# Second attention of a two-layer encoder step: the diagonal mask moves from VectorE's product and the second accumulation into the score accumulation on TensorE

## The chip, the cores and the metric

One core of a Trainium2 chip (trn2). The metric is the device time of one execution in microseconds: the median of several runs, lower is better. The kernel before takes 2124.3 us (median of 3 runs, 2124.23 to 2124.6).

## The reference

One inference step of a two-layer encoder over 1024 prompt rows and 32 sample rows (which see 512 cached rows), width 1024. Layer 0 uses differential attention, layer 1 stick-breaking attention. After each comes an output projection, a gated per-layer embedding, and at the end one rmsnorm. All arithmetic is float32. The change touches only the attention of layer 1, for 16 heads of 64:

```python
def block(qb, qpb):
    z = jnp.einsum('bqhd,bkhd->bhqk', qb.astype(f32), kf) * (B_DH ** -0.5)
    valid = k_pos[None, :] < qpb[:, None]
    log_keep = jnp.where(valid, jax.nn.log_sigmoid(-z), 0.0)
    after = lax.cumsum(log_keep, axis=3, reverse=True) - log_keep
    a = jnp.where(valid, jnp.exp(jax.nn.log_sigmoid(z) + after), 0.0)
    return jnp.einsum('bhqk,bkhd->bqhd', a, vf)
```

A weight is exp(z - the sum of softplus(z) over this key and all later valid ones), and a query sees only keys strictly ahead of it.

## The kernel before, in words

The program runs in phases: a norm, the first attention (names with the prefix la), a mixing phase (mix_a), the second attention (`stick_layer`, prefix lb), a second mixing phase (mix_b). Each phase gives every engine its own hand-written list of instructions, tied together by counting semaphores; there is no scheduler.

`stick_layer` works through eight groups of two heads. Groups 0 to 6 are a hardware loop, group 7 is written out behind it. In a group the keys lie on the 128 partitions and the queries in the free dimension. The work goes by **pairs** (c, b): query chunk c (0 and 1: 512 prompt queries each; 2: the 32 sample rows) against key block b of 128 keys. The order is (0,0) to (0,3), (1,0), (2,0), (1,1) to (1,7), thirteen pairs; a pair has one **unit** for each of the two heads, the sample pair one unit for both. A pair is diagonal where some of its queries lie inside the key block: (0,0) to (0,3) and (1,4) to (1,7). Such a pair computes only the columns from the block on (512, 384, 256 and 128 of them), and its first 128 columns need the strict mask. So 8 x 2 = 16 units of a group are diagonal, and 128 in all.

A unit goes round the engines so:

- TensorE, `scores` (L1496 on, matmul at L1529; sample pair L1520): three products (high x high, low x high, high x low) of 64-row operands, term by term, and within a term head 0 and then head 1. The result is z in a PSUM bank of lb_sc. The semaphore z is raised per head at its last term.
- VectorE, `clamp` (L1286): min(z, 40) into lb_m. ScalarE, `exp` and `log` (L1132, L1137): ln(1 + exp).
- VectorE, `softplus`: max(z, that) into lb_s (L1299), the softplus. In a diagonal unit a second instruction multiplies the first 128 columns by the 0/1 matrix `strict` (L1305), behind a semaphore from the first; in the sample unit it is `strict_sample` (L1310), ahead of sums over the key blocks in lb_rs (L1313, L1316). Then `split` makes a high part (the cast, L1336) and a low part (L1338).
- TensorE, `after`: in a diagonal unit first the **hide** matmul (L1548; sample L1542), which adds -1e30 to the masked entries of z by unit x hide on the full 128 x 128 array; then two triangle matmuls (L1551), which subtract the sums of the softplus. It waits for the semaphore soft ahead of the hide and for low ahead of the triangles. `column_sums` (L1562) adds up a pair's whole softplus.
- ScalarE, `weights` (L1147): exp of the bank into lb_a. TensorE, `values` (L1587; sample L1581): the products with v. VectorE, `add` (L1355), and GpSimd, a scaling by what the block keeps (L1457), gather them in lb_o.

The order on TensorE in step i is: scores of pair i, values of pair i-2, after and column sums of pair i-1, and then, in most steps, a piece of projection (L105): the last token tiles of this group (steps 0 to 2), with small transposes (L1494), the gate (steps 3 to 5), or the first token tiles of the next group (from step 6). VectorE in step i: the clamps of pair i, add of pair i-2, softplus and split of pair i, then gate work, splits of the next group's weights (L1265, steps 3 and 5; L1270) and of turned tiles (L1275). At a group's end come the last add and `finish` (L1365), and then the loop's branch. In group 7 the splits of weights are replaced by splits of the next phase's operand (L1203 on ScalarE, L1407 on VectorE).

SP issues the loads and stores; the mask tables are loaded once, at the start of the program.

In the listing, `views(s)` gives a unit's bank and buffers, `span(c, b)` the first column of a pair, their number, and whether it is diagonal.

Of the kernel before, what the change touches and what calls it, by code (L numbers as in the profile page):

```python
# [27 lines left out]
P = 128  # L28
# [890 lines left out]
def stick_layer(nc, top, name, h, w_in, k_past, v_past, k_out, v_out, o_dram, w_out, ident, masks, stage, norm):  # L919
# [29 lines left out]
        q = max(0, b * P - c * QC)  # L949
        return q, QC - q, b >= 4 * c  # L950

    diagonal = sum(c < 2 and b >= 4 * c for c, b, _ in UNITS)
    with ExitStack() as ctx:
        sb = lambda n, s, dt=F32: ctx.enter_context(nc.sbuf_tensor(f"{name}_{n}", s, dt))
        pb = lambda n, s: ctx.enter_context(nc.psum_tensor(f"{name}_{n}", s, F32))
# [17 lines left out]
                     turned=9, turned_high=9, turned_low=9, past_turned=1, past_high=1, past_low=1,  # L973
                     tok_stored=64, g_ready=3, g_normed=3, g_clamped=3, g_exp=3, g_log=3, g_soft=3, g_sig=3, g_done=3,
                     z=N, clamped=N, exp=N, log=N, soft=N, high=SPLIT, low=SPLIT, after=N, a=N, sums=CARRIED,
                     keep=CARRIED, scaled=CARRIED, added=NP - 1, sampled=1, pv=NP, dve_link=diagonal + 5, o_ready=3,
                     pe_tick=0, fill=1, pads=1)
        table.update({f"w_loaded{s}": 16 * KT // STAGES for s in range(STAGES)})
        table.update({f"o_stored{c}": 16 for c in range(3)})
# [265 lines left out]
        def _(dve):  # L1245
# [32 lines left out]
            def body(r, more):  # L1278
# [7 lines left out]
                    dve.tensor_scalar(x, slot, SOFT_MAX, None, ALU.min).then_inc(S["clamped"], 1)  # L1286

                def softplus(s):
                    c, b, _ = UNITS[s]
                    slot, x, sp, _ = views(s)  # L1290
                    dve.wait_ge(S["log"], at.next("log"))

                    if s < 2:
                        dve.wait_ge(S["low"], at.before("low"))
                    elif UNITS[s - 2][0] == 2:
                        dve.wait_ge(S["after"], at.nth("after", s - 1))
                    else:
                        dve.wait_ge(S["low"], at.nth("low", split_before(s - 1)))
                    ins = dve.tensor_tensor(sp, slot, x, ALU.max)  # L1299
                    if c < 2 and not span(c, b)[2]:  # L1300
                        ins.then_inc(S["soft"], 1)
                    elif c < 2:
                        ins.then_inc(S["dve_link"], 1)
                        dve.wait_ge(S["dve_link"], at.next("dve_link"))
                        dve.tensor_tensor(sp[:, 0:P], sp[:, 0:P], masks["strict"][:, :], ALU.mult).then_inc(S["soft"], 1)  # L1305
                    else:
                        ins.then_inc(S["dve_link"], 1)
                        dve.wait_ge(S["dve_link"], at.next("dve_link"))
                        new = sp[:, :, PB * DEC:]
                        dve.tensor_tensor(new, new, masks["strict_sample"][:, :, :], ALU.mult).then_inc(S["dve_link"], 1)  # L1310
                        dve.wait_ge(S["dve_link"], at.next("dve_link"))
                        dve.wait_ge(S["after"], at.nth("after", s))
                        dve.tensor_copy(rs[:, :, PB - 1, :], new).then_inc(S["dve_link"], 1)  # L1313
                        dve.wait_ge(S["dve_link"], at.next("dve_link"))
                        for b in reversed(range(PB - 1)):
                            ins = dve.tensor_tensor(rs[:, :, b, :], rs[:, :, b + 1, :], sp[:, :, (b + 1) * DEC:(b + 2) * DEC],  # L1316
                                                    ALU.add)
                            if b:
                                ins.then_inc(S["dve_link"], 1)
                                dve.wait_ge(S["dve_link"], at.next("dve_link"))  # L1320
                            else:
                                ins.then_inc(S["soft"], 1)
# [149 lines left out]
        def _(pe):  # L1472
# [24 lines left out]
            def body(r, more):  # L1497
                at, ahead = Count(table, r), Count(table, r + 1)

                def scores(i):  # L1500
                    c, b = PAIRS[i]
                    if i >= 2:
                        pe.wait_ge(S["a"], at.nth("a", through(i - 2)))
                    else:
                        pe.wait_ge(S["a"], at.before("a"))
                    if i == 0:
                        pe.wait_ge(S["turned_low"], at.nth("turned_low", 4))
                    if (c, b) == (1, 0):
                        pe.wait_ge(S["turned_low"], at.nth("turned_low", NT))
                    if c == 2:  # L1510
                        pe.wait_ge(S["turned_low"], at.all("turned_low"))
                        pe.wait_ge(S["past_low"], at.all("past_low"))
                        high, low = qk
                        slot = views(units(i)[0])[0]
                        for b in range(SB):
                            for n, (x, y) in enumerate(((0, high), (1, high), (0, low))):
                                for hd in range(2):
                                    f = slice(hd * DH, (hd + 1) * DH)
                                    keys = kpt[x][f, b * P:(b + 1) * P] if b < PB else qk[x][f, 1, SEQ:]
                                    last = pe.matmul(slot[:, hd, b * DEC:(b + 1) * DEC], keys, y[f, 0, SEQ:ROWS],  # L1520
                                                     start=b == 0 and n == 0, stop=n == 2, skip_group_check=True)
                        last.then_inc(S["z"], 1)
                        return
                    q = span(c, b)[0]
                    high, low = qk
                    for n, (x, y) in enumerate(((high, high), (low, high), (high, low))):
                        for s in units(i):
                            f = slice(UNITS[s][2] * DH, (UNITS[s][2] + 1) * DH)
                            last = pe.matmul(bank(s)[:, q:], x[f, 1, b * P:(b + 1) * P],  # L1529
                                             y[f, 0, c * QC + q:(c + 1) * QC], start=n == 0, stop=n == 2,  # L1530
                                             skip_group_check=True)
                            if n == 2:
                                last.then_inc(S["z"], 1)

                def after(s):
# [3 lines left out]
                    pe.wait_ge(S["soft"], at.nth("soft", s + 1))  # L1539
                    if c == 2:  # L1540
                        for hd in range(2):
                            pe.matmul(slot[:, hd, PB * DEC:], unit[:, :], hide[:, 0:DEC], **add)  # L1542
                            pe.matmul(slot[:, hd, 0:PB * DEC], masks["neg_ones"][:, :],
                                      rs[:, hd].rearrange("p b n -> p (b n)"), **add)
                            last = pe.matmul(slot[:, hd, :], masks["neg_tri"][:, :], sp[:, hd, :], **add)
                    else:
                        if span(c, b)[2]:
                            pe.matmul(slot[:, 0:P], unit[:, :], hide[:, :], **add)  # L1548
                        pe.wait_ge(S["low"], at.nth("low", split_before(s) + 1))
                        for part in halves(s):  # L1550
                            last = pe.matmul(slot, tri[:, :], part, **add)  # L1551
# [629 lines left out]
def build(nc, A, out):  # L2181
# [3 lines left out]
    with top:  # L2185
# [2 lines left out]
        o_dram = internal("o_t", (GROUPS, P, ROWS))  # L2188
        ident = top.enter_context(nc.sbuf_tensor("ident", [P, P], F32))
        masks = {n: top.enter_context(nc.sbuf_tensor(n, s, F32)) for n, s in  # L2190
                 (("neg_tri", [P, P]), ("neg_ones", [P, P]), ("strict", [P, P]), ("strict_sample", [P, 2, DEC]))}
        h_offset = -(-nc.sbuf_base // 32) * 32
        h = [top.enter_context(nc.sbuf_tensor(f"h_{n}", [P, KT, ROWS], F32R)) for n in ("high", "low")]
        stage = top.enter_context(nc.sbuf_tensor("stage", [P, STAGE], F32))
# [74 lines left out]
```

## Time and profile before

| | us |
|---|---|
| median of 3 runs | 2124.3 (2124.23 to 2124.6) |
| the profiled execution | 2126.75 |
| its span in the profile | 2125.0 |
| TensorE busy | 1911.1 |
| VectorE busy | 1255.2 |
| ScalarE busy | 1005.7 |
| GpSimd busy | 323.0 |

The mean granted clock of TensorE in this execution is 0.957 of full speed. Times in the profile count from the start of the span. A timeline row gives the start, the duration, the engine, the line, the operation and its operands; a bracket at its end is the engine's idle time before it and what ended it. Durations of matmuls hold their latency, so that neighbours overlap; what one costs in a dense stretch is the step from its start to the next one's. "x2" is two instructions merged into one row.

### The profile page before, as it was taken

The numbers are of one execution on the slowest core, as the hardware profiler recorded it, in microseconds if no ns is written. First come the engines' busy times: TensorE is split into PE (matmuls) and PEld (weight loads), VectorE is DVE, ScalarE is ACT, GpSimd is POOL, SyncE is SP. The second block draws the span as 40 slices with busy tenths as digits, with TensorE's granted clock in tenths as the row PEclk, the third lists the DMA queues.
The fourth block names the chain that finished last, engine by engine and source line by source line (L and its number), as shares of the span: only waits on it lengthen the run. The fifth ranks groups of instructions, "written<-read, shape, count | busy, mean of one in ns | idle before, by whom it ended". The sixth has DMA issues, their size and how long they took to land. (4 is left out here: it accounts for less than half of the span.)

```text
span 2125.0 us, 35549 instructions
## 1 busy us (share of the span) xinstructions
PE 1911.1 (90%) x11420; PEld 1637.2 (77%) x11420; DVE 1255.2 (59%) x2661; ACT 1005.7 (47%) x2361; POOL 323.0 (15%) x541
## 2 busy tenths in 40 slices
PE   3999989999899889996799999999999999689995
PEld 2877878878778689986777777777777778479995
DVE  4456555564554622454286868686868686844455
ACT  5455454554554622454254555454545454522345
POOL 0111111111111000264010101110101011100341
PEclk7999999999999889998999999999999999979999
DMA  4121111211111232211111111010111111133213
GB/s 130 51 63 49 48 45 56 60 35 45 55 56 49 92 104 84 70 64 57 36 46 36 45 35 55 26 55 25 55 35 45 44 37 46 72 101 96 63 47 122
DMA packets 161891, 124.22 MB, mean 58 GB/s; under 512 B 11136, under 2 KB 152768, under 8 KB 161792
## 3 DMA queue, kind: packets, MB, share of 16 engines
q1 hardware_dynamic: 161792, 123.08, 18.8%
q8 instruction: 40, 0.66, 0.1%
q14 instruction: 59, 0.48, 0.1%
HBM read 89.53 MB, written 33.52 MB: 58 GB/s over the span
## 5 line engine op out<-in xcount | busy, mean ns | idle before, releaser
L105 PE MATMUL lb_pj<-lb_w_high,h_high 128*128 128x384 f32 (+1 forms) x576 | 209.1, 363 | 19.4 <-DVE lb_w_low L1265 10.3
L105 PE MATMUL la_pj<-la_w_high,h_high 128*128 128x384 f32 (+1 forms) x576 | 208.0, 361 | 6.9 <-DVE la_w_low L569 6.9
L1132 ACT ACTIVATE lb_m<-lb_m 128x512 f32<-128x512 f32 (+4 forms) x200 | 98.8, 521 | 236.5 <-DVE lb_m L1286 235.3
L105 PE MATMUL lb_pj<-lb_w_high,h_low 128*128 128x384 f32 (+1 forms) x576 | 200.8, 349 | 0.0
L105 PE MATMUL lb_pj<-lb_w_low,h_high 128*128 128x384 f32 (+1 forms) x576 | 200.0, 347 | 0.0
L105 PE MATMUL la_pj<-la_w_low,h_high 128*128 128x384 f32 (+1 forms) x576 | 195.9, 340 | 0.0
L105 PE MATMUL la_pj<-la_w_high,h_low 128*128 128x384 f32 (+1 forms) x576 | 195.0, 339 | 0.0
L1457 POOL TENSOR_TENSOR lb_o<-lb_o,lb_keep 128x512 f32<-128x512 f32 (+3 forms) x80 | 77.3, 967 | 649.0 <-ACT lb_keep L1156 649.0
L1299 DVE TENSOR_TENSOR lb_s<-lb_sc,lb_m 128x512 f32<-128x512 f32 (+4 forms) x200 | 110.1, 550 | 61.3 <-ACT lb_m L1137 61.2
L418 ACT ACTIVATE la_p<-la_sc,la_nm 128x128 f32<-128x128 f32 (+5 forms) x144 | 106.1, 739 | 57.8 <-DVE la_nm L608 56.0
L105 PEld LDWEIGHTS lb_pj<-lb_w_high,h_high 128*128 128x128 f32 (+1 forms) x576 | 108.4, 188 | 29.4 <-issue 11.7
L1286 DVE TENSOR_SCALAR lb_m<-lb_sc 128x512 f32<-128x512 f32 (+4 forms) x200 | 101.4, 547 | 38.5 <-PE lb_sc L1529 23.0
L1338 DVE TENSOR_TENSOR lb_s_low<-lb_s,lb_s_high 128x512 fp32r<-128x512 f32 (+1 forms) x192 | 113.7, 592 | 6.6
L105 PEld LDWEIGHTS la_pj<-la_w_high,h_high 128*128 128x128 f32 (+1 forms) x576 | 105.3, 183 | 12.6 <-issue 6.8
L105 PEld LDWEIGHTS lb_pj<-lb_w_high,h_low 128*128 128x128 f32 (+1 forms) x576 | 108.5, 188 | 5.8
L105 PEld LDWEIGHTS lb_pj<-lb_w_low,h_high 128*128 128x128 f32 (+1 forms) x576 | 107.8, 187 | 4.3
L606 DVE TENSOR_REDUCE la_mx<-la_sc 128x1 f32<-128x128 f32 (+5 forms) x144 | 107.6, 747 | 3.1 <-DVE la_sc L601 0.2
L105 PEld LDWEIGHTS la_pj<-la_w_low,h_high 128*128 128x128 f32 (+1 forms) x576 | 104.4, 181 | 4.3
L105 PEld LDWEIGHTS la_pj<-la_w_high,h_low 128*128 128x128 f32 (+1 forms) x576 | 105.0, 182 | 3.2
L1551 PE MATMUL lb_sc<-lb_s_high,lb_tri 128*128 128x512 f32 (+1 forms) x192 | 79.5, 414 | 28.5 <-DVE lb_s_low L1338 28.5
L1336 DVE CAST lb_s_high<-lb_s 128x512 fp32r<-128x512 f32 (+1 forms) x192 | 79.8, 416 | 25.1
L1137 ACT ACTIVATE lb_m<-lb_m 128x512 f32<-128x512 f32 (+4 forms) x200 | 92.3, 507 | 0.3
(295 smaller groups left out, 5197.4 us busy)
## 6 DMA issues: line engine op xcount, KB each, us to landing
stage<-in_a_w_in SPq DMA_DIRECT2D x60, 192.0 KB, 3.1
stage<-in_b_w_in SPq DMA_DIRECT2D x60, 192.0 KB, 2.9
stage<-in_ple_w_gate SPq DMA_DIRECT2D x22, 512.0 KB, 3.6
h_low<-o_t SPq DMA_DIRECT2D x14, 528.0 KB, 6.5
mix_b_xs<-x_mid SPq DMA_DIRECT2D x8, 528.0 KB
norm_a_xt<-in_x SPq DMA_DIRECT2D x8, 512.0 KB, 3.6
stage<-in_a_w_in SPq DMA_DIRECT2D x16, 256.0 KB, 5.2
out_ak<-la_tok SPq DMA_DIRECT2D x8, 512.0 KB, 3.3
```

What stands on the lines that cost most here:

```text
L105: last = pe.matmul(out, x, y, start=start and n == 0, stop=stop and n == 2, **kw)
L418: act.activation(p[c][u % (3 - c)][0:n, 0:nk], scores_of(u)[:, c, :], ACT.Exp, bias=nm[0:n, u % 2, c:c + 1], accum_out=sums[0:n, u % 2, c: ...
L606: dve.reduce_max(mx[0:n, u % 2, c:c + 1], x[:, c, :], AX.X).then_inc(S["dve_link"], 1)
L1132: act.activation(x, x, ACT.Exp).then_inc(S["exp"], 1)
L1137: act.activation(x, x, ACT.Ln, bias=1.0).then_inc(S["log"], 1)
L1286: dve.tensor_scalar(x, slot, SOFT_MAX, None, ALU.min).then_inc(S["clamped"], 1)
L1299: ins = dve.tensor_tensor(sp, slot, x, ALU.max)
L1336: dve.tensor_copy(high, sp).then_inc(S["high"], 1)
L1338: dve.tensor_tensor(low, sp, high.bitcast(F32), ALU.subtract).then_inc(S["low"], 1)
L1457: pool.tensor_tensor(out, out, kept[n % 2][:, q:], ALU.mult).then_inc(S["scaled"], 1)
L1551: last = pe.matmul(slot, tri[:, :], part, **add)
```

## The change

The hide matmul moves. For a diagonal pair it is issued in `scores`, for each head right after that head's last term, ahead of the semaphore z; for the sample pair both follow the last score matmul. So z is already about -1e30 in masked entries when it is clamped: exp gives 0, the logarithm 0, and the max 0, which is what the product gave. The products with `strict` and `strict_sample` go, with the semaphore step between max and product, and so does the table `strict_sample`. `after` no longer issues the hide. The numbers of hide matmuls, 128 and 16, stay the same.

```diff
--- before.py
+++ after.py
@@ softplus(s), VectorE
-                    c, b, _ = UNITS[s]
+                    c = UNITS[s][0]
                     slot, x, sp, _ = views(s)
...
                     ins = dve.tensor_tensor(sp, slot, x, ALU.max)
-                    if c < 2 and not span(c, b)[2]:
+                    if c < 2:
                         ins.then_inc(S["soft"], 1)
-                    elif c < 2:
-                        ins.then_inc(S["dve_link"], 1)
-                        dve.wait_ge(S["dve_link"], at.next("dve_link"))
-                        dve.tensor_tensor(sp[:, 0:P], sp[:, 0:P], masks["strict"][:, :], ALU.mult).then_inc(S["soft"], 1)
                     else:
                         ins.then_inc(S["dve_link"], 1)
                         dve.wait_ge(S["dve_link"], at.next("dve_link"))
                         new = sp[:, :, PB * DEC:]
-                        dve.tensor_tensor(new, new, masks["strict_sample"][:, :, :], ALU.mult).then_inc(S["dve_link"], 1)
-                        dve.wait_ge(S["dve_link"], at.next("dve_link"))
                         dve.wait_ge(S["after"], at.nth("after", s))
@@ body(r, more), TensorE
+                masked = dict(start=False, stop=True, skip_group_check=True)
+
                 def scores(i):
...
                                     last = pe.matmul(slot[:, hd, b * DEC:(b + 1) * DEC], keys, y[f, 0, SEQ:ROWS],
                                                      start=b == 0 and n == 0, stop=n == 2, skip_group_check=True)
+                        for hd in range(2):
+                            last = pe.matmul(slot[:, hd, PB * DEC:], unit[:, :], hide[:, 0:DEC], **masked)
                         last.then_inc(S["z"], 1)
                         return
...
                             if n == 2:
+                                if span(c, b)[2]:
+                                    last = pe.matmul(views(s)[0][:, 0:P], unit[:, :], hide[:, :], **masked)
                                 last.then_inc(S["z"], 1)
@@ after(s), TensorE
                     if c == 2:
                         for hd in range(2):
-                            pe.matmul(slot[:, hd, PB * DEC:], unit[:, :], hide[:, 0:DEC], **add)
...
                     else:
-                        if span(c, b)[2]:
-                            pe.matmul(slot[:, 0:P], unit[:, :], hide[:, :], **add)
                         pe.wait_ge(S["low"], at.nth("low", split_before(s) + 1))
```

The rest of the diff is the count of the semaphore dve_link (four steps a group instead of 16 + 5) and the list of mask tables.

## Rows read from the trace of the kernel before

**Rows 1.** The page of the kernel before: busy time of each engine.

```profile
PE 1911.1 (90%) x11420; PEld 1637.2 (77%) x11420; DVE 1255.2 (59%) x2661; ACT 1005.7 (47%) x2361; POOL 323.0 (15%) x541
```

**Rows 2.** Windows, us: PE, PEld, DVE, ACT, POOL busy; granted clock; DMA share; GB/s.

```profile
1140.00:1240.00 100.00, 94.26 (x568) 75.16 (x567) 75.17 (x159) 53.85 (x131) 11.59 (x12) 0.97 0.14 43
1155.00:1170.00 15.00, 11.90 (x53) 9.53 (x50) 10.27 (x23) 5.89 (x16) 0.00 (x0) 0.77 0.10 30
1260.00:1275.00 15.00, 12.15 (x59) 9.90 (x60) 11.39 (x26) 7.06 (x20) 0.00 (x0) 0.89 0.06 20
...
1778.00:1793.00 15.00, 14.04 (x85) 10.71 (x82) 12.55 (x30) 7.70 (x20) 1.03 (x1) 1.00 0.10 26
1840.00:1880.00 40.00, 22.59 (x92) 15.00 (x91) 29.96 (x60) 20.49 (x41) 5.00 (x5) 0.69 0.15 47
```

**Rows 3.** Waits from 1040 to 1880 us: us in total, times, longest.

```profile
PE lb_sc L1551 <- DVE lb_s_low L1338: 28.5, 31, 1.1
```

**Rows 4.** Timeline of TensorE, heads of groups 2 and 7: start us, us.

```profile
1260.76 0.33 PE L1548 MATMUL lb_sc<-lb_hide,lb_unit 128*128 128x128 f32 x1 [1.11 <-DVE lb_s L1305]
1262.02 0.50 PE L1551 MATMUL lb_sc<-lb_s_high,lb_tri 128*128 128x512 f32 x1 [0.93 <-DVE lb_s_low L1338]
...
1264.23 0.50 PE L1551 MATMUL lb_sc<-lb_s_high,lb_tri 128*128 128x512 f32 x1 [0.96 <-DVE lb_s_low L1338]
...
1264.87 0.53 PE L105 MATMUL lb_pj<-lb_w_high,h_high 128*128 128x384 f32 x1
1265.19 0.53 PE L105 MATMUL lb_pj<-lb_w_high,h_low 128*128 128x384 f32 x1
...
1780.32 0.50 PE L1551 MATMUL lb_sc<-lb_s_high,lb_tri 128*128 128x512 f32 x1 [0.96 <-DVE lb_s_low L1338]
```

**Rows 5.** Timeline of VectorE at the head of group 2.

```profile
1257.09 1.29 DVE L1286 TENSOR_SCALAR lb_m<-lb_sc 128x512 f32<-128x512 f32 x2 [2.52 <-issue]
1259.69 0.69 DVE L1299 TENSOR_TENSOR lb_s<-lb_sc,lb_m 128x512 f32<-128x512 f32 x1 [1.32 <-ACT lb_m L1137]
...
1260.81 0.43 DVE L1336 CAST lb_s_high<-lb_s 128x512 fp32r<-128x512 f32 x1
...
1261.88 0.68 DVE L1299 TENSOR_TENSOR lb_s<-lb_sc,lb_m 128x512 f32<-128x512 f32 x1
```

**Rows 6.** Timeline of TensorE in the last group.

```profile
1844.65 0.44 PE L1529 MATMUL lb_sc<-lb_qk_high 64*128 64x384 f32 x2 [4.03 <-ACT lb_a L1147]
```

**Rows 7.** Timeline of VectorE, pair (1,1), not a diagonal one.

```profile
1304.62 0.69 DVE L1299 TENSOR_TENSOR lb_s<-lb_sc,lb_m 128x512 f32<-128x512 f32 x1 [0.62 <-ACT lb_m L1137]
1305.44 0.43 DVE L1336 CAST lb_s_high<-lb_s 128x512 fp32r<-128x512 f32 x1
```

**Rows 8.** Timeline of TensorE, scores and after of pairs (1,3) to (1,5).

```profile
1322.27 0.34 PE L105 MATMUL lb_pj<-lb_w_high,h_low 128*128 128x384 f32 x1
1322.45 0.34 PE L105 MATMUL lb_pj<-lb_w_low,h_high 128*128 128x384 f32 x1
...
1323.05 0.40 PE L1529 MATMUL lb_sc<-lb_qk_high,lb_qk_low 64*128 64x512 f32 x2
1323.28 0.40 PE L1529 MATMUL lb_sc<-lb_qk_low,lb_qk_high 64*128 64x512 f32 x2
...
1324.62 0.50 PE L1551 MATMUL lb_sc<-lb_s_high,lb_tri 128*128 128x512 f32 x1
...
1325.65 0.40 PE L1562 MATMUL lb_pj<-lb_s_high,lb_half 128*128 128x512 f32 x1
...
1332.83 0.33 PE L1548 MATMUL lb_sc<-lb_hide,lb_unit 128*128 128x128 f32 x1
...
1334.09 0.39 PE L1562 MATMUL lb_pj<-lb_s_high,lb_half 128*128 128x512 f32 x1
```

**Rows 9.** Timeline of TensorE, transposes of the sample rows between gate projections.

```profile
1180.08 0.33 PE L105 MATMUL lb_pj<-h_low,lb_wg_high 128*128 128x352 f32 x1
...
1180.84 0.33 PE L105 MATMUL lb_pj<-h_high,lb_wg_low 128*128 128x352 f32 x1
```

More of the change, by code:

```diff
@@ L950, in span @@
         return q, QC - q, b >= 4 * c
-    diagonal = sum(c < 2 and b >= 4 * c for c, b, _ in UNITS)
     with ExitStack() as ctx:
@@ L975, in stick_layer @@
                      z=N, clamped=N, exp=N, log=N, soft=N, high=SPLIT, low=SPLIT, after=N, a=N, sums=CARRIED,
-                     keep=CARRIED, scaled=CARRIED, added=NP - 1, sampled=1, pv=NP, dve_link=diagonal + 5, o_ready=3,
+                     keep=CARRIED, scaled=CARRIED, added=NP - 1, sampled=1, pv=NP, dve_link=4, o_ready=3,
                      pe_tick=0, fill=1, pads=1)
@@ L2190, in build @@
         masks = {n: top.enter_context(nc.sbuf_tensor(n, s, F32)) for n, s in
-                 (("neg_tri", [P, P]), ("neg_ones", [P, P]), ("strict", [P, P]), ("strict_sample", [P, 2, DEC]))}
+                 (("neg_tri", [P, P]), ("neg_ones", [P, P]), ("strict", [P, P]))}
         h_offset = -(-nc.sbuf_base // 32) * 32
```

## The prediction

> **What bounds the kernel now.** The page comes first: over 2125.0 us TensorE is busy 90%, VectorE 59% [rows 1]. The change touches only the second attention (prefix lb), 1050 to 1869 us, eight head groups, so next come the windows: in a steady 100 us of it TensorE is busy 94.26 us and VectorE 75.17 [rows 2]. TensorE is the bound, with holes. The list of waits says what most holes wait for: VectorE's split of the softplus, 28.5 us in 31 waits [rows 3]. The timeline puts them in three places.
>
> (a) The head of groups 1 to 6. TensorE has done the scores of pair 1 at 1259.66 and idles 1.11, 0.93 and 0.96 us ahead of the hide and triangle matmuls of pair 0; from 1264.23 it runs on [rows 4]. It waits for a VectorE chain that starts late: 2.52 us of issue after the loop's branch, clamps, 1.32 us for ScalarE, then max, mask product, cast, subtract, twice [rows 5]. Group 7 isn't entered through that branch and has one hole, of 0.96 us [rows 4]; group 0, behind the prologue, also has one.
>
> (b) Pairs (1,1) and (1,2) of each group. That VectorE chain begins at a gate product which waits for TensorE, and holds the splits of the next weights; no diagonal pair lies in it.
>
> (c) The last group, from 1823 us, where VectorE also prepares the next phase: TensorE waits up to 4.03 us at a time [rows 6], and of the last 40 us VectorE is busy 29.96 [rows 2].
>
> Elsewhere TensorE runs without a hole, and whatever it is given costs its full step.
>
> **VectorE's side.** 128 products and 8 small ones go. What counts of one is the time from the start of the max to the start of the cast: 1260.81 - 1259.69 = 1.12 us with it [rows 5], 1305.44 - 1304.62 = 0.82 without [rows 7]. With the second head's like it, that is 0.31 us per unit, 0.62 per pair.
> - In (a) the pair lies on the path: -0.62 us per group, in six groups.
> - In (c) four diagonal pairs lie on VectorE's path: 4 x 0.6 = 2.4 us, and the tail, where TensorE sets the pace again, loses two pairs of hides, 0.5 (priced below): -2.9 us together. That some products run longer there beside GpSimd I don't count: the next VectorE instruction would meet GpSimd in their place.
> - Elsewhere VectorE has slack, and TensorE's work covers the saving. The small sample product is worth nothing either: behind it VectorE waits for ScalarE's half of the weight split. Without that cover it would be worth at most a unit's 0.31 us, 2.5 over eight groups.
>
> **TensorE's side.** The number of matmuls stays; their place doesn't. Leaving `after`, a pair's two hides give back 0.23 us: from its first matmul to the column sums it is 1334.09 - 1332.83 = 1.26 us with them, 1325.65 - 1324.62 = 1.03 without [rows 8]. In `scores` they cost more, for two reasons.
>
> First, the two heads of a pair now run at once, on 64 rows each: two matmuls of 512 columns take one step of 1323.28 - 1323.05 = 0.23 us [rows 8]. A hide uses all 128 rows and now stands between the last term of head 0 and that of head 1, so this step is paid twice: +0.23 us for 512 columns and, by columns, 0.17, 0.12, 0.06 for 384, 256, 128.
>
> Second, each change between 64-row and 128-row matmuls leaves a bubble. From the last projection to the second score step it is 1323.05 - 1322.45 = 0.60 us; less a projection's step (1322.45 - 1322.27 = 0.18) and a score's 0.23, 0.19 is left [rows 8]. Two tiny transposes on 32 rows between gate projections show a whole detour: 1180.84 - 1180.08 = 0.76 us, less two steps of 0.16 (0.18 x 352/384), leaves 0.44 for out, the two, and back [rows 9]. The new order makes one detour (head 0, hide, head 1) and half of another (head 1, hide; the values switch again, as they do now): 0.66 us, hides included. Bounds: 0.23 if the array switched for free (the hides' own price in `after`), 0.83 if three bubbles of 0.20 came on top of that. I take 0.66, which is nearest to a measured row of the same kind. Net of the 0.23 given back, a pair costs +0.66, 0.60, 0.55, 0.49 us for 512, 384, 256, 128 columns.
>
> The Trainium skill (TensorEngine Tiling (Array Packing), Key Properties) says that changing the tiling mode, and not just the tile, drains the TensorE; it has no figure. By that rule the sum takes the detours; if a switch were no more than a change of tile, it would take the lower bound. The bubbles in the trace agree with the rule.
>
> Where is this paid?
> - Pairs 0 and 1 of groups 1 to 6: their scores grow by 0.89 and 0.83 us, all ahead of (a). Up to the first triangle matmul TensorE would otherwise idle 1.11 + 0.33 (the hide that leaves) + 0.93 - 0.31 = 2.06 us [rows 4], so 1.72 is covered. The mask comes ahead of the clamp now, and clamp, ScalarE and the rest of the chain queue behind it; but pair 0's clamp stands behind 2.52 us of issue, which its scores use up only in part, and later clamps have slack. Pair 1's own hides leave an exposed place: -0.23. So six times -0.62 - 0.23: -5.1 us.
> - Pairs (0,2), (0,3), (1,4) to (1,7): 0.55 + 0.49 + 0.66 + 0.60 + 0.55 + 0.49 = 3.34 us, exposed in groups 0 to 6: +23.4 us.
> - Group 7: (0,2) and (0,3) exposed, +1.0; at its head TensorE overruns the short hole, +0.3; with (c), -2.9: -1.6 in all. Group 0's head: 0, overrun and saving being alike. The sample's hides: in the slack of (b), 0.
> - Queues: SP drops one small load at the start, 0. No other queue is passed, no wait is added.
> Sum so far: +23.4 - 5.1 - 1.6 = +16.7 us.
>
> **The clock.** The hole of (a) costs more than its idle time. Around it the granted clock is 0.77 over 15 us in three of the groups 1 to 6 and 0.89 in the other three, and 1.00 in group 7, with its one hole of 0.96 us [rows 2]. Behind the hole projections step 1265.19 - 1264.87 = 0.32 us instead of 0.18: the 1.2 GHz level [rows 4]. Clock lost: 3 x 0.23 x 15 + 3 x 0.11 x 15 = 15.3 us. In the three groups at 0.77 it falls already inside the last idle stretch; I take 0.4 us off for each: 14.1 us. After the change the mostly idle stretch, now 1259.66 to 1264.23 = 4.6 us with 3.0 idle, begins 1.7 later and ends 0.6 earlier: 2.2 us with some 1.5 idle, in holes of about 0.3 and 1.2. I expect all six drops to go: -14.1 us. Bounds: 0 (all stay) and -15.3.
>
> **Sum:** 16.7 - 14.1 = +2.6 us. The profiled execution took 2126.75 us (span 2125.0), 2.45 above the median of the runs, 2124.3; the difference is applied to the median: 2127 us, +0.13%. A measurement here tells 0.2%, 4.2 us, from no change.
>
> **Rivals.**
> 1. Switching is cheap, faster. A pair costs +0.23, 0.17, 0.12, 0.06 net. Exposed: 7 x 0.87 = +6.1; heads -5.1; last group about -2.7. With less work ahead of (a) the low stretch is 3.0 us, and I let a third of the drops stay: -9.4. Total -11 us: 2113; with bubbles at half, 2119. For: bubbles are inferred from starts, not seen. Against: two different detours give the same 0.2. Chance with its neighbours 0.26.
> 2. The clock drops stay, slower. Place: the head of groups 1 to 6. The hides, part of the little work inside the hole, leave it, and what idling remains may still be enough. Price: +16.7 with all drops (2141), +9.7 with half (2134). It decides from the point where more than one of the six groups still shows 0.89 or less. For: now all six drop. Against: the idle time there more than halves. With it I count dearer switches (0.83 instead of 0.66: +7 us, 2134, drops gone). Together 0.34.
> 3. The change does little: a hide costs the same in either place and the clock stays as it is; savings of 8 us stand against as much head-splitting, within 2 us of 2124. This (0.08) and the forecast (0.32) make 0.40.
>
> **Range and chances.** The low end, 2114, is rival 1's; the high end, 2137, lies between half and all of the drops staying. Beyond lie free switches with every drop gone, and all drops staying or half of them with dear switches: some 2 in 10. Faster by over 0.2%: 0.26; within 0.2%: 0.40; slower: 0.34.
>
> **What would show it.** (1) From the last score step to the values it is now 0.33 us at 512 columns; that part grows by 0.9 us in a diagonal pair, with a hide between the two heads' last terms. (2) Max to cast is 0.82 us at 512 columns in every pair, and `after` of a diagonal pair takes 1.03. (3) At the heads of groups 1 to 6 two holes, about 0.3 and 1.2 us, and a clock of 1.00 in the 15 us. (4) Groups of one loop come equally far apart, not in two kinds. (5) The last 40 us of the phase shrink by 2 to 3. The forecast is wrong if the scores of diagonal pairs grow by under 0.5 us at 512 columns, or if the clock still reads 0.89 or less at more than one head.

## The result and the profile after

The changed kernel takes 2146.45 us (median of 4 runs, 2143.62 to 2148.84); the kernel before, run beside it, 2124.45 (4 runs, 2124.23 to 2128.74). The ratio is 1.0098, with a 95% interval of 1.0082 to 1.0114: slower by 1%, and above the range of 2114 to 2137. The profiled execution took 2146.06 us, with a span of 2144.3.

The page of the changed kernel, busy time of each engine, against [rows 1]:

```profile
PE 1949.2 (91%) x11420; PEld 1659.7 (77%) x11420; DVE 1226.7 (57%) x2525; ACT 1009.9 (47%) x2361; POOL 322.4 (15%) x541
```

VectorE has lost 136 instructions and 28.5 us. TensorE has as many matmuls as before and is busy 38.1 us longer: the rearrangement, not an addition, made it dearer.

**Where in the span.** The first matmul of the sample pair's scores is a mark that each group has once. Between the first and the last such mark seven periods pass: 722.3 us before, 741.8 after. Of the 20.0 us by which mix_b's first matmul comes later (1876.39, now 1896.41), those periods hold 19.5; what lies ahead of them, the earlier phases included, 2.0; the stretch from the last mark to mix_b gives 1.4 back (69.14, now 67.74). Of the 2.0, 1.4 come ahead of the second attention, where nothing was changed: in the twelve kernels profiled here its first score matmul starts anywhere from 1049.0 to 1055.1 us, so a difference of 1 or 2 us there says nothing on an edit.

| us between marks, groups | 0-1 | 1-2 | 2-3 | 3-4 | 4-5 | 5-6 | 6-7 |
|---|---|---|---|---|---|---|---|
| before | 104.44 | 103.34 | 103.07 | 104.45 | 103.23 | 104.68 | 99.12 |
| after | 106.40 | 106.03 | 107.47 | 106.60 | 106.43 | 106.05 | 102.82 |

**Step 1, the scores.** The timeline of TensorE in the changed kernel: first the head of group 2 (pair (0,1)'s scores and pair (0,0)'s triangles, against [rows 4]), then a diagonal pair of 512 columns later in the group (against [rows 8]).

```profile
1266.78 0.33 PE L1526 MATMUL lb_sc<-lb_qk_low,lb_qk_high 64*128 64x384 f32 x1
1267.04 0.33 PE L1531 MATMUL lb_sc<-lb_hide,lb_unit 128*128 128x128 f32 x1
1267.29 0.44 PE L1526 MATMUL lb_sc<-lb_qk_low,lb_qk_high 64*128 64x384 f32 x1
1267.66 0.33 PE L1531 MATMUL lb_sc<-lb_hide,lb_unit 128*128 128x128 f32 x1
1268.24 0.50 PE L1547 MATMUL lb_sc<-lb_s_high,lb_tri 128*128 128x512 f32 x1 [0.25 <-DVE lb_s_low L1331]
...
1270.13 0.79 PE L1547 MATMUL lb_sc<-lb_s_high,lb_tri 128*128 128x512 f32 x1 [1.15 <-DVE lb_s_low L1331]
...
1271.14 0.52 PE L105 MATMUL lb_pj<-lb_w_high,h_high 128*128 128x384 f32 x1
1271.46 0.52 PE L105 MATMUL lb_pj<-lb_w_high,h_low 128*128 128x384 f32 x1
...
1330.09 0.39 PE L1526 MATMUL lb_sc<-lb_qk_low,lb_qk_high 64*128 64x512 f32 x1
1330.41 0.33 PE L1531 MATMUL lb_sc<-lb_hide,lb_unit 128*128 128x128 f32 x1
1330.67 0.50 PE L1526 MATMUL lb_sc<-lb_qk_low,lb_qk_high 64*128 64x512 f32 x1
1331.10 0.33 PE L1531 MATMUL lb_sc<-lb_hide,lb_unit 128*128 128x128 f32 x1
1331.35 1.08 PE L1583 MATMUL lb_acc<-lb_a,lb_tok 128*64 128x512 f32 x4
1332.36 0.50 PE L1547 MATMUL lb_sc<-lb_s_high,lb_tri 128*128 128x512 f32 x1
...
1333.40 0.39 PE L1558 MATMUL lb_pj<-lb_s_high,lb_half 128*128 128x512 f32 x1
```

From the last term of head 0 to the values it is 1331.35 - 1330.09 = 1.26 us; from the last term to the values it was 0.33. That is +0.93, less the 0.23 that `after` gives back: +0.70 net, where the prediction had 0.66. At 384, 256 and 128 columns the same reading gives +0.88, 0.82 and 0.76, net 0.65, 0.59 and 0.53, against 0.60, 0.55 and 0.49. `after` of the pair takes 1333.40 - 1332.36 = 1.04 (predicted 1.03).

**Step 2, VectorE.** The timeline of VectorE in the changed kernel, last group:

```profile
1864.87 0.69 DVE L1298 TENSOR_TENSOR lb_s<-lb_sc,lb_m 128x512 f32<-128x512 f32 x1 [0.62 <-ACT lb_m L1136]
1865.69 0.43 DVE L1329 CAST lb_s_high<-lb_s 128x512 fp32r<-128x512 f32 x1
...
1866.76 0.68 DVE L1298 TENSOR_TENSOR lb_s<-lb_sc,lb_m 128x512 f32<-128x512 f32 x1
1867.57 0.87 DVE L1329 CAST lb_s_high<-lb_s 128x512 fp32r<-128x512 f32 x1
```

Max to cast is 0.82 and 0.81 us, as predicted. The second cast runs 0.87 instead of 0.43, as the product did at this place in the kernel before (0.65 instead of 0.29), both beside a scaling on GpSimd: that cost went to the next instruction, as the prediction assumed. Once it grew on the way: in pair (1,5) a subtract takes 1.59 us instead of 0.56, where the product had taken 0.88.

**Step 3, the heads and the clock.** Group 2's two holes are 0.25 and 1.15 us (0.22 to 0.45 and 1.15 to 1.16 in the six groups), as forecast. But the triangle at 1270.13 already takes 0.79 us where the one at 1332.36 takes 0.50 at full clock, and projections step 0.32: the 1.2 GHz level. The windows of the changed kernel (us; PE, PEld, DVE, ACT, POOL busy; granted clock; DMA share; GB/s), against [rows 2]: heads of groups 1 to 3, 10 us in the middle of group 3, head of group 4, head of group 7, the end of the phase.

```profile
1161.00:1176.00 15.00, 13.39 (x63) 10.52 (x64) 10.63 (x24) 7.32 (x18) 0.22 (x1) 0.89 0.01 4
1268.00:1283.00 15.00, 13.61 (x67) 10.68 (x68) 10.81 (x23) 7.00 (x17) 1.01 (x1) 0.89 0.00 1
1374.00:1389.00 15.00, 13.63 (x59) 11.18 (x59) 9.60 (x22) 6.88 (x17) 0.00 (x0) 0.77 0.00 1
1410.00:1420.00 10.00, 10.00 (x52) 8.37 (x51) 7.72 (x16) 7.02 (x17) 0.95 (x1) 0.85 0.00 1
1482.00:1497.00 15.00, 13.74 (x66) 10.95 (x67) 10.63 (x23) 7.00 (x17) 1.02 (x1) 0.89 0.00 1
...
1800.00:1815.00 15.00, 15.00 (x86) 11.35 (x87) 10.00 (x22) 7.49 (x19) 1.01 (x1) 1.00 0.00 1
...
1860.00:1900.00 40.00, 27.83 (x99) 17.88 (x96) 29.96 (x53) 20.70 (x41) 4.88 (x5) 0.67 0.15 48
```

All six heads still show 0.89 or less (groups 5 and 6, not shown, 0.89 as well), five at 0.89 and one at 0.77; before it was three and three. And one drop is new, at 1410, where TensorE doesn't idle at all. By the periods of the kernels whose head holes are filled (e5 and e6 below), the low stretches cost 12.4 us before and 10.3 now, over six periods each: 2.1 less, not 14.1.

**Against the total.** Scores 7 x (0.70 + 0.65 + 0.59 x 2 + 0.53 x 2) = 7 x 3.59 = +25.1 (pairs (0,2), (0,3), (1,4) to (1,7)); a further 7 x 0.23 = +1.6, since the 0.23 that pair (0,3) gives back falls into the slack of (b) and saves nothing (the holes there sit 0.2 us later after their mark than before). The rest is what the periods leave over and no separate check: heads -5.0 (the filled kernels e5 and e6 below, 2.99 - 3.82 = -0.83 each, where the prediction has -0.85); clock -2.1; group 7's head -0.1 (3.70 - 3.82). Together that is the 19.5 measured.

### The profile page after: what moved, and what is told of

Read it like the earlier page. It is cut to its first block and busy times, and to the rows that moved or that the text cites. A ratio compares the mean times of both kernels' runs of the same rounds, so it can differ in the third digit from the quotient of the medians.

```text
span 2144.3 us, 35309 instructions
## 1 busy us (share of the span) xinstructions
PE 1949.2 (91%) x11420; PEld 1659.7 (77%) x11420; DVE 1226.7 (57%) x2525; ACT 1009.9 (47%) x2361; POOL 322.4 (15%) x541
## 5 line engine op out<-in xcount | busy, mean ns | idle before, releaser
L1131 ACT ACTIVATE lb_m<-lb_m 128x512 f32<-128x512 f32 (+4 forms) x200 | 101.4, 522 | 231.8 <-DVE lb_m L1285 230.5
L1329 DVE CAST lb_s_high<-lb_s 128x512 fp32r<-128x512 f32 (+1 forms) x192 | 108.2, 563 | 27.7 <-DVE lb_s L1298 3.5
L1547 PEld LDWEIGHTS lb_sc<-lb_s_high,lb_tri 128*128 128x128 f32 x192 | 37.7, 197 | 86.6 <-issue 54.0
```

What stands on the lines that cost most here:

```text
L1131: act.activation(x, x, ACT.Exp).then_inc(S["exp"], 1)
L1329: dve.tensor_copy(high, sp).then_inc(S["high"], 1)
```

## Experiments

All ratios are to the kernel before, run on the same chip beside them; the times differ by a few us between the three sets of runs (e1 to e4, e5 to e8, e9 and e10; medians of before: 2127.3, 2126.9, 2129.3), so ratios are compared and not times. "Period" is the time between marks, as above.

### e1_products_gone: one half of the change, the products alone

The kernel before, with `after` still issuing the hides:

```diff
-                    elif c < 2:
-                        ins.then_inc(S["dve_link"], 1)
-                        dve.wait_ge(S["dve_link"], at.next("dve_link"))
-                        dve.tensor_tensor(sp[:, 0:P], sp[:, 0:P], masks["strict"][:, :], ALU.mult).then_inc(S["soft"], 1)
...
-                        dve.tensor_tensor(new, new, masks["strict_sample"][:, :, :], ALU.mult).then_inc(S["dve_link"], 1)
```

> Kernel before without VectorE's products; the hide matmuls stay in `after`. Left out: the mask of the softplus in diagonal blocks and in the sample block, so keys that a query must not see are summed in its softplus sums. It is VectorE's half of the change alone. Theory A (the change costs TensorE about 25 us in the scores, and VectorE's side gives about 6): the six heads of groups lose 0.62 us each and the last group 2.4, together 5 to 7 us below before (2118), with the clock drops still there. Rival B (the product is on no path that counts): within 2 us of before. Rival C (a shorter hole keeps the clock up): 2110 or less, granted clock 1.00 at the heads.

Measured: 2117.34 us (6 runs, 2115.29 to 2120.29), ratio 0.995 (0.9933 to 0.9967). The products' price was real: the periods of groups 1 to 6 are 102.48 to 102.67, the tail, from the last mark to mix_b, is 2.2 us shorter than before (2.4 predicted of the products). The whole gain, 10 us, is more than the 5 to 7 expected: all six heads still drop, but all to 0.89 and none to 0.77, so a part of it is the clock's. So the 1% is not VectorE's; against this kernel the hide's move costs some 1.5%.

### e2_hide_moved_only: the other half

```diff
                     elif c < 2:
                         ins.then_inc(S["dve_link"], 1)
+                        dve.wait_ge(S["dve_link"], at.next("dve_link"))
+                        dve.tensor_tensor(sp[:, 0:P], sp[:, 0:P], masks["strict"][:, :], ALU.mult).then_inc(S["soft"], 1)
```

The changed kernel with the products put back.

> The changed kernel with VectorE's products kept: only the hide matmuls move. It is TensorE's half alone. Theory A: 25 us for scores in groups 0 to 6, 1.4 less for hides that leave the exposed place behind the heads, nothing from VectorE: 22 to 28 us above before (2146 to 2152), and at least as slow as the changed kernel by 3 to 6 us. Rival D (the changed kernel is slow because VectorE's shorter chain collides with something, such as GpSimd): 2130 or less.

Measured: 2155.93 us (4 runs, 2151.42 to 2157.59), ratio 1.013 (1.0104 to 1.0155). The halves add up: +1.3% for the move, -0.5% for the products, +1.0% for both within the intervals. The move is the loss.

### e3_hides_behind_both: one detour instead of one and a half, and no split heads

Over the changed kernel:

```diff
-                            if n == 2:
-                                if span(c, b)[2]:
-                                    last = pe.matmul(views(s)[0][:, 0:P], unit[:, :], hide[:, :], **masked)
+                            if n == 2 and not diagonal:
                                 last.then_inc(S["z"], 1)
+                    if diagonal:
+                        for s in units(i):
+                            pe.matmul(views(s)[0][:, 0:P], unit[:, :], hide[:, :], **masked).then_inc(S["z"], 1)
```

> The changed kernel, but in a diagonal pair both hides follow the last term of both heads, so the heads still run at once and the array switches to 128 rows only once more. Theory A (cost is the doubled last term and the switches between 64 and 128 rows): from the last score step to the values 0.68 us instead of 1.26 at 512 columns and 0.33 before; net of what leaves `after` +0.12 us per pair, +5 us in all, against 6 to 7 gained: 2121 to 2126, some 22 us under the changed kernel. Rival E (the slowness is that z is raised later and VectorE starts its chain late): head 0's z comes as late as before this edit, so 2140 or more.

Measured: 2128.47 us (10 runs, 2123.26 to 2131.16), ratio 1.0003 (0.9991 to 1.0015). The timeline of TensorE in this kernel, pair (1,4):

```profile
1326.71 0.40 PE L1527 MATMUL lb_sc<-lb_qk_low,lb_qk_high 64*128 64x512 f32 x2
1327.04 0.44 PE L1534 MATMUL lb_sc<-lb_hide,lb_unit 128*128 128x128 f32 x2
1327.41 1.08 PE L1585 MATMUL lb_acc<-lb_a,lb_tok 128*64 128x512 f32 x4
```

The last term of both heads to the values is 0.70 us, where the changed kernel has 1.26: 0.56 us a pair come from the order alone, with the same matmuls. By the prediction's pricing 0.23 of that is the 512-column step paid twice and the rest the second way out and back; the two were not tried apart. This kernel's head holes are larger than the changed kernel's (1.29 to 1.59 and 1.06 to 1.16 us), since its scores fill less of the wait, and six heads still drop. Head 0's z comes as late here as in the changed kernel, so a late z (rival E, 2140 or more) is not what makes that one slow. It came out some 2 us above the 2121 to 2126 expected; in the profile three further drops stand in the middle of groups (at 1090, 1404 and 1612).

### e4_hides_first: the hides open the accumulation

Over the changed kernel (the sample pair likewise):

```diff
+                    if diagonal:
+                        for s in units(i):
+                            pe.matmul(views(s)[0][:, 0:P], unit[:, :], hide[:, :], start=True, stop=False, ...)
...
-                                             y[f, 0, c * QC + q:(c + 1) * QC], start=n == 0, stop=n == 2,
+                                             y[f, 0, c * QC + q:(c + 1) * QC], start=n == 0 and not diagonal,
```

> The changed kernel, but the hides open the accumulation, ahead of the scores, while the array is in 128-row mode anyway from the projection before. No extra switch, no doubled term. Theory A: hides cost in scores what they gave back in `after` (0.23 us a pair), and only VectorE's gain is left: 6 to 8 us below before, 2116 to 2118, the fastest of the four, if the clock drops stay; 14 us less again if they go. Rival E (late z): z is raised at the same place as in the kernel before plus 0.2 us, so about before. Rival F (any place in the scores costs more, because the 64-row matmuls behind a hide start late): 2125 to 2135.

Measured: 2113.51 us (4 runs, 2111.35 to 2115.03), ratio 0.9934 (0.9911 to 0.9957): 14 us below before, where 6 to 8 were expected with the drops there and 14 more without them; four of the six heads drop. The timeline of TensorE in this kernel, the head of group 2 and then pair (1,4):

```profile
1258.60 0.33 PE L1526 MATMUL lb_sc<-lb_hide,lb_unit 128*128 128x128 f32 x2
...
1260.98 0.50 PE L1549 MATMUL lb_sc<-lb_s_high,lb_tri 128*128 128x512 f32 x1 [1.32 <-DVE lb_s_low L1331]
...
1262.87 0.79 PE L1549 MATMUL lb_sc<-lb_s_high,lb_tri 128*128 128x512 f32 x1 [1.15 <-DVE lb_s_low L1331]
...
1322.22 0.34 PE L105 MATMUL lb_pj<-lb_w_low,h_high 128*128 128x384 f32 x1
1322.39 0.33 PE L1526 MATMUL lb_sc<-lb_hide,lb_unit 128*128 128x128 f32 x2
1322.66 0.50 PE L1530 MATMUL lb_sc<-lb_qk_high 64*128 64x512 f32 x2
...
1323.23 0.39 PE L1530 MATMUL lb_sc<-lb_qk_low,lb_qk_high 64*128 64x512 f32 x2
1323.55 1.08 PE L1585 MATMUL lb_acc<-lb_a,lb_tok 128*64 128x512 f32 x4
```

From the last projection to the last score step it is 1.01 us, against 0.83 in the kernel before [rows 8]: both hides add 0.18, and `after` gives 0.23 back. Placed between full-array projections and the scores, the hide stands where the switch to 64 rows is paid anyway. (That the later columns may be written by a matmul that doesn't open an accumulation is what the Trainium skill states in PSUM — Partial Sum Buffer, Terms: without the opening flag a matmul accumulates where the written bit is set and overwrites where it is clear. No trace here shows the bit itself.)

The windows of this kernel at the heads of groups 1 to 4 price a drop inside one kernel:

```profile
1151.00:1166.00 15.00, 12.46 (x75) 10.57 (x74) 8.16 (x16) 6.95 (x16) 0.00 (x0) 1.00 0.27 89
1259.00:1274.00 15.00, 12.53 (x58) 10.44 (x59) 9.93 (x20) 6.45 (x17) 0.00 (x0) 0.77 0.07 20
1363.00:1378.00 15.00, 12.51 (x73) 9.71 (x72) 12.10 (x26) 7.87 (x21) 1.01 (x1) 1.00 0.07 21
1465.00:1480.00 15.00, 13.67 (x70) 11.03 (x71) 10.71 (x24) 6.99 (x18) 1.01 (x1) 0.89 0.00 1
```

The periods around them are 100.77, 103.50, 100.68 and 102.22: a drop to 0.89 costs 1.6 us and one to 0.77 2.8 us, close to the 1.65 and 3.05 of the prediction's arithmetic. Its price per drop was right; whether the drops go was not.

### e5_before_filled, e6_after_filled, e7_first_filled: the clock taken out

Useless matmuls of 384 columns into a bank that is free then, in groups 0 to 6, ahead of the two `after` calls at a head (5 and 5 over the kernel before; 1 and 5 over the changed kernel; 7 and 5 over the hides-first kernel):

```diff
+                def warm(count):
+                    pe.wait_ge(S["added"], at.before("added"))
+                    for _ in range(count):
+                        pe.matmul(acc[:, 0:384], tri[:, :], w[0][:, 0, :], start=True, stop=True, ...)
...
                         for s in units(i - 1):
+                            if i == 1 and more:
+                                warm(5 if s == 0 else 5)
                             after(s)
```

> The kernel before, with five matmuls of 384 columns without use (into the bank lb_acc, which the values overwrite later) ahead of `after` of each unit of pair 0, in groups 0 to 6. The five take 0.9 us each time and lie inside a hole in which TensorE waits for VectorE (in group 0 the hole is shorter, up to 1 us is lost there). Theory A with G (low activity of TensorE around the head brings the clock down, at 1.7 us a drop, 3 for a long one): granted clock 1.00 at the heads of groups 1 to 6, 8 to 14 us below before. Rival H (the clock drops for a reason outside the holes, or the drops cost nothing since later holes absorb them): no change, or 1 to 3 us slower for the added work.

> The changed kernel with the same useless matmuls in its holes: one ahead of unit 0 of pair 0 and five ahead of unit 1, groups 0 to 6. Theory G: the clock stays up at the heads, 9 to 13 us below the changed kernel, about 2134 to 2138; what is left against before is TensorE's cost in the scores less VectorE's gain. It is the time that the prediction should have given with its drops gone. Rival H: at the changed kernel's 2146 or above.

> The hides-first kernel with seven and five useless matmuls in its two holes. Theory G: clock 1.00 at the heads, groups 100.7 us apart throughout (now 100.7, 102.3 or 103.5), 5 to 9 us below the hides-first kernel: 2105 to 2109. Rival H: 2113 or above.

Measured: e5 2116.58 us (5 runs, 2113.46 to 2117.37), ratio 0.9948 (0.9931 to 0.9965); e6 2140.57 (4 runs, 2136.95 to 2141.84), ratio 1.0062 (1.0039 to 1.0085); e7 2111.61 (4 runs, 2110.25 to 2112.49), ratio 0.9923 (0.99 to 0.9946). None of the 18 heads drops any more; one window of the kernel before, filled, at the head of group 2:

```profile
1255.00:1270.00 15.00, 13.39 (x78) 10.87 (x76) 11.74 (x26) 7.67 (x18) 0.00 (x0) 1.00 0.22 68
```

Matmuls that compute nothing make the kernel before 10 us faster. And the pair e5 and e6 prices the change with no head drop on either side: 2140.57 - 2116.58 = +24.0 us, where the prediction's sum without the clock is +16.7. By periods, the filled kernels go from 101.67-101.93 to 104.71-104.95 (without the one of 105.33, which holds a drop in its middle), +3.0 a group where the prediction has 3.34 - 0.85 = +2.5, and the seventh from 99.17 to 103.15. Of the 24, some 2.6 come ahead of the first mark, 1.8 of them ahead of the second attention, where the profiles differ by more than that although no edit lies there.

The changed kernel, filled, still drops twice, and not at a head. Its window after the sample scores of group 2, and its timeline there:

```profile
1298.00:1308.00 10.00, 10.00 (x70) 8.48 (x68) 8.10 (x19) 4.84 (x11) 0.95 (x1) 0.83 0.00 1
```

```profile
1299.11 0.26 PE L1515 MATMUL lb_sc<-lb_qk_low,lb_qk_high 64*128 64x32 f32 x2
1299.30 0.40 PE L1518 MATMUL lb_sc<-lb_hide,lb_unit 128*128 128x32 f32 x2
...
1300.33 0.39 PE L1547 MATMUL lb_sc<-lb_s_low,lb_tri 128*128 128x512 f32 x1
...
1300.93 0.63 PE L1547 MATMUL lb_sc<-lb_s_low,lb_tri 128*128 128x512 f32 x1
1301.36 0.49 PE L105 MATMUL lb_pj<-h_high,lb_wg_high 128*128 128x352 f32 x1
1301.65 0.49 PE L105 MATMUL lb_pj<-h_high,lb_wg_low 128*128 128x352 f32 x1
```

There is no bracket in these rows: TensorE had no idle time. Before the clock fell it had done 1.8 us of sample scores (two matmuls of 64 rows and 32 columns every 0.11 us), the sample's hides and two switches. So the granted clock can fall behind thin work (few rows, few columns) as well as behind idle time. The new drop in the middle of the changed kernel's group 3 stands at the same place, and the traces of all kernels say what it takes. Nine such drops are in them, all 2.6 to 3.5 us behind the mark, and all in the four kernels that issue the sample pair's hides behind its scores: one in the changed kernel, three in e2, three in e3, two in e6. The other eight have the same sample scores without hides behind them and not one such drop. It costs little, some 0.6 us in e6's 105.33, since the slack of (b) follows.

### e8_first_products_kept: hides first, with the products put back

> The hides-first kernel with VectorE's products kept: only the place of the hides differs from the kernel before. Theory A: scores plus `after` of a diagonal pair cost the same within 0.1 us, so the time is that of before less some 1.4 us (the hides of pair 1 leave the exposed place behind the heads) and less a little for the scores, 2120 to 2127; and 7 to 14 us above the hides-first kernel, which is what VectorE's half gives. Rival F (a hide in the scores always costs more): 2130 or more.

Measured: 2126.17 us (10 runs, 2121.19 to 2129.32), ratio 0.9993 (0.998 to 1.0005). Beside the hides-first kernel's 0.9934, the products are worth 0.6% here, as they are in e1 (0.5%); a part of it is the clock, since here all six heads drop and in the hides-first kernel four. The head holes are 1.66 to 1.86 and 1.48 us.

### e9_first_hole_filled, e10_second_hole_filled: which hole lets the clock fall

The hides-first kernel, with six useless matmuls ahead of unit 0's triangles only, or five ahead of unit 1's only (as diffs over e7):

```diff
-                                warm(7 if s == 0 else 5)
+                                warm(6 if s == 0 else 0)
...
-                                warm(7 if s == 0 else 5)
+                                warm(0 if s == 0 else 5)
```

> The hides-first kernel with six useless matmuls ahead of unit 0 only. What is left idle at a head is then what the changed kernel has, some 0.3 and 1.15 us, but ahead of it stand dense 128-row matmuls instead of scores with bubbles and single heads. Theory K (in the changed kernel the clock still falls because the scores of pair 1, thinned by the switches, join the holes as time of low activity): the clock stays at 1.00 at all six heads, about 2111 as with both holes filled. Theory L (the second hole of 1.15 us with its surroundings is enough by itself): drops at most of the six heads, 0.89, and 2117 or more.

> The mirror of it: five useless matmuls ahead of unit 1 only, so that the first hole of 1.3 us stays and the second shrinks to 0.3. The idle time left is the same as in the run before, in the other place. If only the sum of idle time around the head counts, and not which hole it is, both runs show the same clock: 1.00 at the heads, about 2111. Theory L: clock 1.00 here, 0.89 in the other.

Measured: e9 2106.41 us (4 runs, 2103.79 to 2108.07), ratio 0.9895 (0.9878 to 0.9913); e10 2105.25 (4 runs, 2100.65 to 2109.79), ratio 0.9886 (0.9865 to 0.9908). The timeline of TensorE in e9, head of group 2, and its window there:

```profile
1259.83 1.31 PE L1555 MATMUL lb_acc<-lb_w_high,lb_tri 128*128 128x384 f32 x6
1261.23 0.50 PE L1549 MATMUL lb_sc<-lb_s_high,lb_tri 128*128 128x512 f32 x1
...
1263.11 0.50 PE L1549 MATMUL lb_sc<-lb_s_high,lb_tri 128*128 128x512 f32 x1 [1.15 <-DVE lb_s_low L1331]
...
1263.68 0.34 PE L105 MATMUL lb_pj<-lb_w_high,h_high 128*128 128x384 f32 x1
1263.86 0.34 PE L105 MATMUL lb_pj<-lb_w_high,h_low 128*128 128x384 f32 x1
```

```profile
1259.00:1274.00 15.00, 13.76 (x82) 10.67 (x81) 11.92 (x25) 8.29 (x22) 0.69 (x1) 1.00 0.09 26
```

The hole of 1.15 us is there, the very size that the changed kernel has behind its 0.25, and none of the six heads drops. In e10 the first hole stays (1.33 to 1.66 us) and the second is at most 0.28; two of six drop, where either theory had one clock for all six. By heads, each from one profiled execution:

| kernel | idle at a head, us | heads of six with a drop |
|---|---|---|
| before | 0.96-1.25, 0.93, 0.81-0.96 | 6 |
| products gone (e1) | 0.62-0.93, 0.93, 0.96 | 6 |
| hides behind both (e3) | 1.29-1.59, 1.06-1.16 | 6 |
| hides first, products kept (e8) | 1.66-1.86, 1.48 | 6 |
| hides first (e4) | 1.32-1.41, 1.15 | 4 |
| **changed** | **0.22-0.45, 1.15** | **6** |
| hides first, second hole filled (e10) | 1.33-1.66, up to 0.28 | 2 |
| hides first, first hole filled (e9) | up to 0.30, 1.15-1.17 | 0 |

The changed kernel idles less than e4 or e10 at a head and yet drops more often. What it has more of is thin work ahead of the hole: in the rows of group 2 above, from 1266.78 to 1268.24, there are two score terms of single heads and two hides of 128 columns with a switch before each. In e9 six dense 384-column matmuls stand at that place. That fits the reading that it is the work ahead of a hole that decides, but doesn't prove it. The heads of one kernel follow each other at nearly equal distances, so that six of them are not six independent trials, and no run moved a head in time and left its work as it was. e9 against e10 is not told apart as a time, only as a clock. Both are about 1.1% faster than the kernel before and 2% faster than the changed one; e4, 0.7% faster, needs no useless work.

## Why the prediction was wrong

**The step that failed** is "I expect all six drops to go: -14.1 us". Six drops stayed, with one more in a group's middle: -2.1. The working had sized the idle time well (holes of "about 0.3 and 1.2", measured 0.25 and 1.15) and then took idle time for the cause. That e1 loses idle time too and keeps all six drops, and that the same hole of 1.15 us with dense work ahead (e9) holds the clock, says that idle time alone doesn't decide. The likely reason is that the very work that was to fill the hole is thin. Rival 2 named this outcome with its mark, more than one of six heads at 0.89 or less, and its price of 2141; it was given too little, and the reason that it offered ("what idling remains may still be enough") was at best half of it.

The Trainium skill (TensorE: Matmul & The Clock Gate, HAM oscillation — how this bites in real kernels) warns of a long idle gap as what lets the clock fall. The rows here go beyond that: the longest hole at the changed kernel's heads is 1.16 us, and in e6 the clock falls without any.

**Terms that were mis-sized,** nearly all the same way:

- Scores: +23.4 predicted, +25.1 measured, 0.04 to 0.05 us in each pair. The 0.66 for one and a half detours was right to 6%.
- Pair (0,3)'s give-back of 0.23 a group was counted as time won, while it lies ahead of the slack of (b): +1.6. The prediction had named that slack and still took the credit.
- The tail: -2.9 predicted, -1.4 measured. The products alone give -2.2 (e1); the hides take some 0.8 of it back, where the forecast has them give 0.5. Of the 0.8, 0.3 are there already at pair (1,2), 0.2 come with the subtract of 1.59 us, and 0.3 in the last pairs.
- Group 7's head: +0.3 predicted, -0.1 by its period.

Ahead of the first mark the forecast has +1.0, pairs (0,2) and (0,3) of group 0; the profile has 2.0 there, of which 1.4 lie in phases that the change doesn't touch. 2.0 + 19.5 - 1.4 are, but for rounding, the 20.0 by which mix_b starts later. One slip stands in rival 1: its pairs add up to 0.76 a group and not 0.87, 0.8 us in its total, which decides nothing.

**What held.** The products (e1: both their place and their 0.62 a pair); two different detours giving the same 0.2 a switch, so rival 1 is out (it has +0.23 net at 512 columns, measured +0.70), and with it rival 3; the hole sizes; the price of a drop; max to cast. Of the forecast's marks (1) and (2) came true, (3) in its holes but not in its clock, (4) not (106.03 to 107.47 us from group 1 on, before the last), (5) in half.

With the right clock the prediction would have said 16.7 - 2.1 = +14.6 us, 2139; measured are +22.0. Of the 7.4 between them the terms above explain some 4.4 (1.7 + 1.6 + 1.5 - 0.4), and the rest is of the size by which the time ahead of the second attention differs between profiles.

**A better order** was in reach: nothing in the trace of before argued against the hide ahead of the first term, where full-array projections end and a switch is paid anyway. The Trainium skill (TensorEngine Tiling (Array Packing), Key Properties: a change of tiling mode drains the engine) already points there. e3 and e4 put numbers to it: 0.56 us a pair for gathering the hides, and down to 0.18 for both of them where they stand first, against 0.93 in the changed kernel (at 512 columns).

**What stays open.** How thin the work has to be, and how much of it, before a given hole costs the clock: the six heads of e4 and e10 are alike in holes and differ in drops. Whether in the changed kernel it is the single heads or the switches that do it was not tried apart. And the moment at which a head comes was not varied by itself, so that it may have a part in these counts.

## What to carry to other kernels

Count the changes between 64-row and 128-row matmuls as work of their own (some 0.2 us each here), and put a full-array matmul where such a change is paid anyway: at the start of the accumulation, next to other full-array work, never between the two heads of a packed pair. When a head of a loop shows a low granted clock, don't forecast its return from less idle time alone; ask what stands ahead of the hole, and count on the drops staying until a run says otherwise. And a saving counts only if no slack lies between it and the next thing that is late.

## What was not expected of the hardware

- The clock falls without idle time: 0.83 over 10 us at 1298 in e6, with TensorE busy 10.00 of them, behind sample scores of 64 rows x 32 columns and two hides; nine such drops in four kernels, none in the eight without hides at that place.
- Useless matmuls in a hole pay: 10 of them at each of seven heads take the kernel before from 2126.9 to 2116.6 us.
- With five useless matmuls in the second hole (e10) four of six heads keep the clock, though the first hole is up to 1.66 us; without them (e4) two do.
